# A transformer layer's MLP without GpSimd: the second matrix product taken one Strassen-Winograd product at a time over the whole contraction

## The chip, the cores and the metric

The kernel runs on one core of a Trainium2 chip. A core has a matrix engine (TensorE, PE in the rows), a vector engine (VectorE, DVE), a scalar engine (ScalarE, ACT), a general-purpose engine (GpSimd, POOL), a sync engine (SyncE, SP) that issues the DMAs here, an on-chip memory SBUF (128 partitions) and the accumulators PSUM (8 banks of 128 x 512 float32). Each engine works through its own instructions in order; engines wait for one another on semaphores. PEld in the rows is the matrix engine's weight load, which overlaps its matmuls. The metric is the device time of one execution in microseconds (us), the median of several runs.

## What is computed

One encoder layer on 1024 tokens of width 1024 in float32: neighbourhood attention, a layer norm, and then the part that the change touches:

```python
x   = layer_norm(DN_ALPHA * x + mix, ln1_g, ln1_b)
hid = square(relu(x @ w_ff1))                       # 1024 -> 4096
ple = sigmoid(x @ w_ple_gate) * (p @ w_ple_proj)
x   = layer_norm(DN_ALPHA * x + hid @ w_ff2 + ple, ln2_g, ln2_b)   # 4096 -> 1024
```

## The kernel before

Every float32 operand of a matmul is split in a high part (ScalarE copies it into the matmul's format) and a low part (VectorE subtracts: source minus high). Each product of two tiles is three matmuls (`PASSES`: high x high, high x low, low x high). So before every stretch of matmuls stand pairs "high on ScalarE, low on VectorE".

The function `mlp` has three stages, written out by hand for every engine, so each engine's order is that of the code.

The gate stage computes x @ w_ple_gate in 16 units (8 token tiles by 2 column halves) of 24 matmuls (`gate`, L2125). Per unit ScalarE takes the sigmoid (L1668) and VectorE does two operations (L1913, L1915). Beside it GpSimd forms the combinations of quarters of x that the next stage needs: `x_combinations`, 8 additions or subtractions of 128x512 for each of 4 chunks, 32 in all (L1548, L1558). Each result is split, low part on VectorE at L1881 (`x_low`). After unit 6, VectorE also makes the low parts of the second half of the gate weights (`low`, L1864, 128x1024 each), for which unit 8 waits.

The first product, x @ w_ff1, uses a Strassen-Winograd scheme: 7 products of quarter blocks instead of 8. It goes in 16 units; a unit has 7 products of 12 matmuls (L2165), in the order `UNIT_STEPS` = (1, 4, 5, 6, 2, 7, 3), where product 4 is that of the unit before. VectorE reads products out of PSUM and adds (`plus`, L1930), forms sums of the squared hidden blocks (`hidden_sum`, L1935), and makes the low parts of the next unit's weights (`w1_low`, L1887). GpSimd forms four 128x512 sums of weight blocks per unit (`sums_1_3`, `sums_2_4`, L1584 and L1548). Product 7 of a unit starts only after VectorE has read product 6 out of the same bank. The hidden blocks and their combinations go to DRAM (`S.hid`).

The second product, hid @ w_ff2, is again the 7-product scheme. The contraction of 4096 is cut in 4 "cubes" of 1024. Before, the order is cube by cube: step n is product `PRODUCTS[n % 7]` = (1, 2, 5, 3, 6, 7, 4) of cube n // 7, 28 steps of 4 token tiles (t) of 12 matmuls (L2203). Each step loads 1 MB of hidden blocks (`load_hidden`), splits one 128x2048 weight block (`w2_high` L1706, `w2_low` L1894) and four 128x512 hidden tiles (`hid_high` L1721, `hid_low` L1899). After every one of the 112 (step, tile) pairs VectorE adds the bank into y or `shared_sum` in SBUF (`add_product`, L2011, 4 first ones are copies, L1998). Products marked `CONTINUES` accumulate on the bank of the product before them. The weights are loaded once, 4 blocks of 1 MB per cube, and GpSimd forms the four weight sums per cube, 128x2048 each (L1548). At the last cube it also adds `shared_sum` to three quarters of y (`merge`, L1614, 12 operations).

The layer norm of tiles 0 to 3 starts when step 25 is added. The last two steps, 26 and 27, are interleaved by tile (`STEP_ORDER`). Tiles 4 to 7 use `statistics`, `variance`, `scale`, `offset`, and at the end gain and shift: the gain on VectorE (`times_gain`) or GpSimd, the shift mostly on GpSimd (L1647). VectorE's order at the end (L2063 to L2111) has additions of the last two steps between norm operations. The output goes out in 8 DMAs of one tile (512 KB).

VectorE's main loop of the second product:

```python
for n in range(STEPS2 - 2):
    w2_low(n + 1)
    for t in range(PAIR_TILES):
        hid_low(n + 1, t)
        if n == STEPS2 - 3 and t == PAIR_TILES - 1:
            w2_low(n + 2)
        add_product(n, t)
```

So during step n of the matrix engine VectorE prepares step n + 1. The parts of step n + 1 go into the buffers of step n - 1, so ScalarE's high parts wait until the matmuls of step n - 1 have read them.

Of the kernel before, what the change touches and what calls it, by code (L numbers as in the profile page):

```python
# [1147 lines left out]
def load_gate(sp, S, w_gate, half, i):  # L1148
# [32 lines left out]
STEP_AT = {step: at for at, step in enumerate(STEP_ORDER)}  # L1181

A11, A12, A21, A22, HS1, HS2, HS3, HS4 = range(8)
STAGED = {1: A11, 2: A12, 5: HS1, 3: HS4, 6: HS2, 7: HS3, 4: A22}


def mlp(nc, S, w_ff1, w_ff2, ln_g, ln_b, w_gate, out):

    with ExitStack() as ctx:
# [3 lines left out]
        def sem(name):  # L1193
# [18 lines left out]
        shared_sum = at("shared_sum", [P, PAIR_TILES, HALF], S.act_at + 32 * KB)  # L1212
        gain = at("ln2_gain", [P, D], S.act_at + 48 * KB)
        shift = at("ln2_shift", [P, D], S.act_at + 52 * KB)
        squares = at("ln2_squares", [P, 2, D], free + 48 * KB)

        last_w2 = at("w_ff2_last", [P, 2, KH4, HALF], free + 104 * KB, F32R)
        last_hid = at("hidden_last", [P, 2, 2, KH4, P], S.act_at + 56 * KB, F32R)
        hid_in = [S.raw[:, 0:2, :].rearrange("p a (b n) -> p (a b) n", n=HALF),
                  at("hidden_in", [P, KH4, HALF], free + 16 * KB)[:, :, :]]  # L1220
        w2_in = [S.raw[:, 2:4, :].rearrange("p a (b n) -> p (a b) n", n=HALF),
                 at("w_ff2_in_1", [P, KH4, HALF], free + 24 * KB)[:, :, :],
                 at("w_ff2_in_2", [P, KH4, HALF], free + 48 * KB)[:, :, :],
                 at("w_ff2_in_3", [P, KH4, HALF], free + 56 * KB)[:, :, :],
                 at("w_ff2_in_4", [P, KH4, HALF], S.act_at + 40 * KB)[:, :, :]]
# [35 lines left out]
        b_in = [sem(f"w_ff2_in{i}") for i in range(5)]  # L1261
# [3 lines left out]
        t2_lo = sem("w_ff2_lo_done")  # L1265
        s2_hi = sem("hidden_hi_done")
# [14 lines left out]
        last_ready = sem("out_last_ready")  # L1281
# [5 lines left out]

        X_STEPS = {1: (0, 1), 2: (2, 3), 3: (4,), 4: (5, 6), 5: (7, 8), 6: (9,), 7: (10,), 8: (11, 12), 9: (13,), 10: (14, 15)}

        EARLY_STEPS = (11, 12)  # L1290
# [66 lines left out]
        def hid_part(part, n, t):  # L1357

            if n % 2 == 0:
                return columns(early_slot(part, t) if t < 2 else wb_slot(part, 2 + t))  # L1360
            if n == STEPS2 - 1:
                return last_hid[:, part, t % 2] if t < 2 else xc[2][:, part, :, P * t:P * (t + 1)]
            if t < 2:
                return columns(wb_slot(part, 6 + t))
            return xc[2][:, part, :, P * (t - 2):P * (t - 1)]

        def w2_part(part, n):

            if n == STEPS2 - 1:
                return last_w2[:, part, :, :]  # L1370
# [4 lines left out]
        def w2_roles(b):  # L1375

            role = {A11: 0, A21: 1, A12: 2, A22: 3, "sum": 4}
            for _ in range(b):
                role = {A11: role[A11], A21: role[A22], A12: role["sum"], "sum": role[A12], A22: role[A21]}
            return role  # L1380

        def w2_loads(slot, b):

            return sum(w2_roles(i)[q] == slot for i in range(b + 1) for q in (A11, A12, A21, A22))
# [9 lines left out]
        def done2(n, t):  # L1394

            return STEP_AT[n, t] + 1

        def bank2(n, t):

            b, i = divmod(n, len(PRODUCTS))  # L1400
            return S.ps[PAIR_TILES * ((3 * b + CHAIN[PRODUCTS[i]]) % 2) + t][:, :]
# [6 lines left out]
        LAST_CUBE = CUBES - 1  # L1408
        MERGE_ORDER = (A22, A12, A21)

        OUT_ORDER = (0, 1, 2, 3, 4, 5, 7, 6)
        DVE_GAINS = 4

# [823 lines left out]
```

## Time and profile before

| | before |
|---|---|
| median of 3 runs | 1352.24 us (1350.94 to 1352.26) |
| the profiled execution | 1351.9 us, its span 1350.1 us |
| mean granted clock of the matrix engine | 0.972 |
| busy: PE, PEld, DVE, ACT, POOL | 1260.3, 1044.9, 912.5, 576.8, 372.3 us |
| first matmul of the gate stage, of the second product | 602.84, 1010.06 us |
| data moved | 174.89 MB, mean 130 GB/s |

The span is that of the profiled execution, from its first to its last instruction; 1.8 us lie around it. All stages named above stand in the last 750 us of the span. A stall of the matrix engine is shown in square brackets in the timeline, with the instruction that ended it.

### The profile page before, as it was taken

What the parts mean: (1) busy time and instruction counts of PE and PEld (TensorE: products, weight loads), DVE (VectorE), ACT (ScalarE), POOL (GpSimd) and SP (SyncE); (2) the same over time, 40 slices, a digit from 0 to 9 for tenths busy, and PEclk for the clock granted to TensorE, in tenths of its full rate; (3) what the DMA queues carried; (4) which work ended last, traced back from release to release, by engine and by line L of the source; (5) the groups of instructions that cost most, each with busy time, mean ns of one, the idle gap of its engine ahead of it and who ended that gap; (6) DMA issues with size and microseconds to landing.
All of it is one profiled execution on the core that took longest, in us unless ns stands there. A gap on an engine that the chain in (4) does not pass through costs nothing. (4 is left out here: it accounts for less than half of the span.)

```text
span 1350.1 us, 18089 instructions
## 1 busy us (share of the span) xinstructions
PE 1260.3 (93%) x5840; PEld 1044.9 (77%) x5840; DVE 912.5 (68%) x1665; ACT 576.8 (43%) x1103; POOL 372.3 (28%) x206
## 2 busy tenths in 40 slices
PE   4999999999999879979899999999999999999992
PEld 3778878878888667868688888888877888888872
DVE  3157766767677646568746666566649788787977
ACT  3145546546555651122324444444443333333352
POOL 0202112112111212129423322233205030222825
PEclk9999999999999899989999999999999999999996
DMA  7313222232223475444354444444456734545114
GB/s 177 83 45 75 69 56 52 66 81 51 66 51 94 147 214 139 136 166 158 125 164 160 143 158 163 142 145 160 164 197 231 273 126 164 167 140 184 63 63 125
DMA packets 120653, 174.89 MB, mean 130 GB/s; under 512 B 10112, under 2 KB 62464, under 8 KB 120576
## 3 DMA queue, kind: packets, MB, share of 16 engines
q1 hardware_dynamic: 120576, 173.95, 41.2%
q8 instruction: 37, 0.61, 0.2%
q14 instruction: 40, 0.33, 0.1%
HBM read 115.20 MB, written 50.52 MB: 123 GB/s over the span
## 5 line engine op out<-in xcount | busy, mean ns | idle before, releaser
L736 PE MATMUL bank<-act_T_hi,w_qkv_hi 128*128 128x512 f32 x384 | 153.7, 400 | 5.6 <-DVEq L689 4.6
L736 PE MATMUL bank<-act_T_hi,w_qkv_lo 128*128 128x512 f32 x384 | 153.8, 401 | 0.0
L736 PE MATMUL bank<-act_T_lo,w_qkv_hi 128*128 128x512 f32 x384 | 153.5, 400 | 0.0
L541 ACT ACTIVATE probabilities<-negated_scores,negated_max 128x384 f32<-128x384 f32 (+1 forms) x128 | 75.5, 590 | 172.0 <-DVE negated_max L669 171.5
L455 POOL TENSOR_TENSOR w_qkv_lo<-weight_raw,w_qkv_hi 128x1024 fp32r<-128x1024 f32 x22 | 52.9, 2403 | 298.0 <-ACT w_qkv_hi L504 298.0
L2165 PE MATMUL bank<-x_combination,weight_parts 128*128 128x512 f32 x480 | 112.9, 390 | 0.0
L2165 PEld LDWEIGHTS bank<-x_combination,weight_parts 128*128 128x128 f32 x480 | 90.1, 188 | 19.0 <-DVE hidden_staging L1930 0.4
L2125 PE MATMUL bank<-weight_parts,act_T_hi 128*128 128x512 f32 x256 | 83.9, 407 | 8.8 <-DVE weight_parts L1864 5.1
L736 PEld LDWEIGHTS bank<-act_T_hi,w_qkv_hi 128*128 128x128 f32 x384 | 73.4, 191 | 18.5 <-DVE w_qkv_lo L227 4.8
L2203 PE MATMUL bank<-weight_parts,weight_parts_early 128*128 128x512 f32 x336 | 80.5, 396 | 3.4 <-DVE weight_parts_early L1899 2.7
L736 PEld LDWEIGHTS bank<-act_T_hi,w_qkv_lo 128*128 128x128 f32 x384 | 73.5, 191 | 13.1
L736 PEld LDWEIGHTS bank<-act_T_lo,w_qkv_hi 128*128 128x128 f32 x384 | 73.5, 191 | 12.8
L2011 DVE TENSOR_TENSOR y<-bank,y 128x512 f32<-128x512 f32 x96 | 65.6, 683 | 23.6 <-PE bank L2203 23.5
L2203 PE MATMUL bank<-weight_parts 128*128 128x512 f32 x336 | 78.7, 390 | 0.4 <-DVE weight_parts L1899 0.4
L676 DVE RECIPROCAL total_reciprocal<-exp_total 128x1 f32<-128x1 f32 x128 | 21.0, 164 | 85.9 <-ACT probabilities L541 85.5
L2203 PEld LDWEIGHTS bank<-weight_parts,weight_parts_early 128*128 128x128 f32 x336 | 64.0, 191 | 17.9 <-issue 4.5
L1548 POOL TENSOR_TENSOR w_ff_in<-w_ff_in,w_ff_in 128x2048 f32<-128x2048 f32 x12 | 58.8, 4900 | 57.5 <-DMA w_ff_in<-in_w_ff 31.2
L650 DVE TENSOR_TENSOR prob_T_lo<-bank,prob_T_hi 128x256 fp32r<-128x256 f32 (+2 forms) x160 | 68.5, 445 | 8.1 <-ACT prob_T_hi L532 6.8
L2203 PEld LDWEIGHTS bank<-weight_parts 128*128 128x128 f32 x336 | 63.0, 188 | 13.8 <-issue 0.8
L2203 PE MATMUL bank<-x_combination,weight_parts 128*128 128x512 f32 x312 | 72.8, 389 | 0.0
L2203 PE MATMUL bank<-x_combination,x_combination 128*128 128x512 f32 x312 | 72.8, 389 | 0.0
L1751 ACT ACTIVATE hidden_staging<-hidden_staging 128x512 f32<-128x512 f32 x48 | 30.3, 632 | 90.7 <-DVE hidden_staging L1930 90.7
(226 smaller groups left out, 3092.4 us busy)
## 6 DMA issues: line engine op xcount, KB each, us to landing
hidden_combinations<-hidden_staging SPq DMA_DIRECT2D x112, 256.0 KB, 2.0
weight_raw<-in_w_ff SPq DMA_DIRECT2D x20, 1024.0 KB, 5.6
weight_raw<-hidden_combinations SPq DMA_DIRECT2D x14, 1024.0 KB, 5.3
hidden_in<-hidden_combinations SPq DMA_DIRECT2D x14, 1024.0 KB, 5.3
weight_raw<-in_na_w_qkv SPq DMA_DIRECT2D x24, 512.0 KB, 4.4
w_ff_in<-in_w_ff SPq DMA_DIRECT2D x12, 1024.0 KB, 7.8
x_tokens<-in_x SPq DMA_DIRECT2D x8, 512.0 KB, 11.3
bias_in<-rpb_rows SPq DMA_DIRECT2D x256, 6.0 KB
```

The costliest lines, as they stand in the source:

```text
L455: nc.gpsimd.tensor_tensor(w[1][:, slot, :, :], S.raw[:, kind, :].rearrange("p (k n) -> p k n", k=KC), w[0][:, slot, :, :].bitcast(F32), AL ...
L541: nc.scalar.activation(prob[:, u % 4, 0:n], score[:, u % 2, 0:n], ACT.Exp, scale=-1.0, bias=nmax[:, u % 4:u % 4 + 1], accum_out=total[:, u ...
L650: last = nc.vector.tensor_tensor(pT_part(pT[1], g, first, count), tile_ps[u % 2][:, at * P:(at + count) * P].rearrange("p (b q) -> p b q", ...
L676: nc.vector.reciprocal(recip[:, u % 4:u % 4 + 1], total[:, u % 4:u % 4 + 1]).then_inc(recip_done, 1)
L736: mm = nc.tensor.matmul(proj_ps[gi % 2][:, :], w[wp][:, (par + kind) % 2, k, :], S.act[ap][:, k, t * HALF:(t + 1) * HALF], start=(i == 0), ...
L1548: nc.gpsimd.tensor_tensor(dst, a, b, ALU.subtract).then_inc(count, 1)
L1751: nc.scalar.activation(stage[:, q, :], stage[:, q, :], ACT.Relu).then_inc(relu_done, 1)
L2011: nc.vector.tensor_tensor(dst, bank2(n, t), dst, ALU.add).then_inc(added, 1)
L2125: mm = nc.tensor.matmul(S.ps[6 + u % 2][:, :], S.act[ap][:, k, t * P:(t + 1) * P], wb_slot(wp, k), start=(k == 0 and n == 0), stop=(k == K ...
L2165: mm = nc.tensor.matmul(bank, w1_part(wp, u, p)[:, k, :], x_part(ap, p, k), start=(k == 0 and n == 0 and p in (1, 5, 6)), stop=(k == KH4 - ...
L2203: mm = nc.tensor.matmul(bank2(n, t), hid_part(ap, n, t)[:, k, :], w2_part(wp, n)[:, k, :], start=(k == 0 and i == 0 and p not in CONTINUES ...
```

## The change

GpSimd has no work left in `mlp`. Its 32 combinations of x go to VectorE, in three groups per chunk after the two operations of a gate unit (`x_first`, `x_second`, `x_third`, with `x_low` between them); units 6, 7, 14 and 15 have none. The first two low parts of unit 0's weights move from gate units 11 and 12 to 14 and 15. The four weight sums of each of the 16 units of the first product go to VectorE: `sums_1_3(u + 2)` at the end of an iteration, `sum_2(u + 1)` ahead of the reading of product 5, `sum_4(u + 1)` ahead of that of product 7. For unit 0 they stand among the low parts between the gate stage and the first unit.

The second product's order is turned round: product by product, and within a product the 4 cubes one after the other, accumulated in PSUM. Step n is product `PRODUCTS[n // 4]`, cube n % 4. A bank is read once per product and tile: 20 additions for products 2, 5, 3, 6, 7; product 1 is copied to `shared_sum` by ScalarE (4 copies); product 4 is read in 4 additions at the end. The weight blocks are loaded again for each product that needs them: 36 loads of 1 MB instead of 16 (`B_LOADS`), through 4 buffers, issued 3 steps ahead. The 16 weight sums of 128x2048 and the 12 merges of 128x512 go to VectorE, behind the second hidden tile of steps 6 to 21 and behind steps 4, 5 and 12. The last product (steps 24 to 27) goes tile by tile: a step is one token tile over all 4 cubes, 48 matmuls, with all four weight parts held; its hidden tiles are loaded in pieces of 512 bytes. The norm of tiles 0 to 3 is laid into steps 21 to 26, that of tiles 4 to 6 into the steps behind theirs. Gain and shift of all tiles are on VectorE, and the last tile goes out in two halves. The number of matmuls stays.

```diff
-STEP_ORDER = tuple((n, t) for n in range(STEPS2 - 2) for t in range(PAIR_TILES)) + tuple(
-    (STEPS2 - 2 + i, t) for i, t in ((0, 0), (0, 1), (1, 0), (0, 2), (1, 1), (0, 3), (1, 2), (1, 3)))
+LAST_FROM = STEPS2 - CUBES
+B_BLOCKS = {1: (A11,), 2: (A21,), 5: (A12, A11), 3: (A22,), 6: (A22, A21), 7: (A22, A12), 4: ()}
+B_LOADS = [(n, q) for n in range(LAST_FROM) for q in B_BLOCKS[PRODUCTS[n // CUBES]]]
...
 # SyncE
+                if n + 3 < LAST_FROM:
+                    for q in B_BLOCKS[PRODUCTS[(n + 3) // CUBES]]:
+                        load_w2(n + 3, q)
...
 # VectorE, gate stage
-                for j in X_STEPS.get(u, ()):
-                    x_low(j)
+                if x_ends(u) is not None:
+                    x_low(4 * x_ends(u) + 3)
+                if x_stage(u):
+                    k, i = x_stage(u)
+                    if i == 0:
+                        x_first(k)
+                    elif i == 1:
+                        x_second(k)
+                    else:
+                        x_third(k)
...
+            sum_2(0)
+            w1_low(0, 2)
+            w1_low(0, 3)
+            sum_4(0)
+            w1_low(0, 4)
+            w1_low(0, 5)
...
 # VectorE, first product
                     w1_low(0, 6)
+                    sums_1_3(1)
...
                     ahead(u + 1, 1)
+                    if u < LAST_UNIT:
+                        sum_2(u + 1)
...
+                    if u < LAST_UNIT:
+                        sum_4(u + 1)
...
+                    if u + 2 < UNITS1:
+                        sums_1_3(u + 2)
...
 # VectorE, second product
+            for n in range(STEPS2):
+                if n + 1 < LAST_FROM:
+                    w2_low(n + 1)
...
+                reads = n % CUBES == CUBES - 1 and CUBES <= n < LAST_FROM
+                for t in range(PAIR_TILES):
+                    if n + 1 < STEPS2:
+                        hid_low(n + 1, t)
+                    if t == 1:
+                        if n in (6, 7, 8, 9):
+                            b_sum_5(n - 6)
...
+                        elif n in (18, 19, 20, 21):
+                            b_sum_7(n - 18)
+                        if n in (15, 16, 17, 18):
+                            b_sum_4(n - 15)
+                    if reads:
+                        add_product(n, t)
+                if n in (4, 5, 12):
+                    merge({4: A22, 5: A12, 12: A21}[n])
...
+                if n >= LAST_FROM:
+                    t = PAIR_TILES + n - LAST_FROM
+                    add_product(n, t - PAIR_TILES)
+                    statistics(t, 0)
+                    variance(t)
...
 # TensorE, last product
+            for t in range(PAIR_TILES):
+                n = LAST_FROM + t
+                free_bank(4, t)
+                for b in range(CUBES):
+                    pe.wait_ge(last_lo, LAST_PARTS.index(b) + 1)
+                    pe.wait_ge(s2_lo, prepared(n, b))
+                    product(bank2(4, t), n, b, lambda part: last_part(part, b), False, b == CUBES - 1, 4)
```

## Rows read from the trace of the kernel before

**Rows 1.** Waits of PE by releaser, 500 to 1350 us: total us, times, longest us
```profile
PE bank L2125 <- DVE weight_parts L1864: 5.1, 2, 4.6
PE bank L2125 <- DVE weight_parts L1869: 3.6, 1, 3.6
...
PE bank L2203 <- issue: 6.8, 2, 5.3
...
PE bank L2165 <- DVE hidden_staging L1930: 1.9, 1, 1.9
```

**Rows 2.** Busy by windows: us, PE, PEld, DVE, ACT, POOL (instructions), PEclk, DMA share, GB/s
```profile
850.00:900.00 50.00, 50.00 (x223) 41.41 (x221) 30.51 (x43) 24.09 (x45) 12.30 (x9) 1.00 0.47 158
...
1045.00:1056.00 11.00, 11.00 (x50) 9.09 (x50) 11.00 (x15) 4.00 (x5) 0.00 (x0) 1.00 0.90 303
```

**Rows 3.** Timeline of PE, gate stage: start, us, what [idle before <- releaser]
```profile
602.84 0.79 PE L2125 MATMUL bank<-weight_parts,act_T_hi 128*128 128x512 f32 x1 [3.61 <-DVE weight_parts L1869]
...
611.18 0.56 PE L2125 MATMUL bank<-weight_parts,act_T_lo 128*128 128x512 f32 x1
...
656.02 0.76 PE L2125 MATMUL bank<-weight_parts,act_T_hi 128*128 128x512 f32 x1 [4.57 <-DVE weight_parts L1864]
...
659.14 0.48 PE L2125 MATMUL bank<-weight_parts,act_T_lo 128*128 128x512 f32 x1
```

**Rows 4.** Timeline of DVE, gate stage and start of the first product
```profile
625.21 1.78 DVE L1913 TENSOR_TENSOR hidden_staging<-hidden_staging 128x512 f32<-128x512 f32 x1
...
653.59 5.62 DVE L1864 TENSOR_TENSOR weight_parts<-weight_raw,weight_parts 128x1024 fp32r<-128x1024 f32 x3
...
702.18 0.69 DVE L1913 TENSOR_TENSOR hidden_staging<-hidden_staging 128x512 f32<-128x512 f32 x1 [4.02 <-ACT hidden_staging L1668]
...
711.04 1.28 DVE L1930 TENSOR_TENSOR hidden_staging<-bank,first_product 128x512 f32<-128x512 f32 x2
```

**Rows 5.** Timeline, start of the second product, POOL and DVE
```profile
1017.20 4.60 POOL L1548 TENSOR_TENSOR w_ff_in<-w_ff_in,weight_raw 128x2048 f32<-128x2048 f32 x1 [37.52 <-DMA w_ff_in<-in_w_ff]
1017.53 4.83 DVE L1899 TENSOR_TENSOR weight_parts<-hidden_in,weight_parts 128x512 fp32r<-128x512 f32 x1
```

**Rows 6.** Timeline of PE, last unit of the first product and the second product
```profile
1000.17 0.84 PE L2165 MATMUL bank<-x_combination,act_T_hi 128*128 128x512 f32 x2 [1.87 <-DVE hidden_staging L1930]
...
1010.06 5.60 PE L2203 MATMUL bank<-weight_parts,weight_parts_early 128*128 128x512 f32 x24
1015.50 5.60 PE L2203 MATMUL bank<-weight_parts 128*128 128x512 f32 x24
...
1037.70 4.58 PE L2203 MATMUL bank<-weight_parts,weight_parts_early 128*128 128x512 f32 x12 [2.01 <-DVE weight_parts_early L1899]
...
1325.91 5.46 PE L2203 MATMUL bank<-w_ff_last,x_combination 128*128 128x512 f32 x12 [5.28 <-issue]
```

**Rows 7.** Timeline of DVE, a norm without POOL work, and the last instruction
```profile
595.26 1.28 DVE L880 SCALAR_TENSOR_TENSOR x_tile<-x_tile,ln_mean_var,ln_gain 128x1024 f32<-128x1024 f32 x1
...
596.65 1.41 DVE L887 SCALAR_TENSOR_TENSOR x_tile<-x_tile,ln_mean_var,ln_shift 128x512 f32<-128x512 f32 x2
...
1344.74 1.23 DVE L2111 TENSOR_TENSOR y<-y,ln_shift 128x1024 f32<-128x1024 f32 x1
```

**Rows 8.** Groups by line: count | busy us, mean ns of one | idle before
```profile
L2011 DVE TENSOR_TENSOR y<-bank,y 128x512 f32<-128x512 f32 x96 | 65.6, 683 | 23.6 <-PE bank L2203 23.5
...
L1894 DVE TENSOR_TENSOR weight_parts<-weight_raw,weight_parts 128x2048 fp32r<-128x2048 f32 x2 | 4.6, 2292 | 6.5 <-ACT weight_parts L1706 6.5
```

**Rows 9.** DMA issues: count, KB each, median us from issue to landing
```profile
hidden_combinations<-hidden_staging SPq DMA_DIRECT2D x112, 256.0 KB, 2.0
weight_raw<-in_w_ff SPq DMA_DIRECT2D x20, 1024.0 KB, 5.6
...
weight_raw<-in_na_w_qkv SPq DMA_DIRECT2D x24, 512.0 KB, 4.4
...
w_ff_in<-in_w_ff SPq DMA_DIRECT2D x12, 1024.0 KB, 7.8
```

More of the change, by code:

```diff
@@ L1260, in mlp @@
         a_in = [sem(f"hidden_in{i}") for i in range(2)]
-        b_in = [sem(f"w_ff2_in{i}") for i in range(5)]
+        b_in = [sem(f"w_ff2_in{i}") for i in range(len(b_raw))]
         y_in = {q: sem(f"y_in{q}") for q in (A11, A12, A21, A22)}
@@ L1373, in w2_part, with last_part, raw_of, loads_of @@
             return xc[0][:, part, :, :]
[L1375 to L1384, printed above, removed]
+        def last_part(part, b):
+            return w2_buffer(part, {0: 0, 3: 1}[b]) if b in (0, 3) else last_w2[b][:, part, :, :]
+        def raw_of(n, q):
+            return b_raw[B_LOADS.index((n, q)) % len(b_raw)]
+        def loads_of(n, q):
+            j = B_LOADS.index((n, q))
+            return b_in[j % len(b_raw)], 16 * (j // len(b_raw) + 1)
+        def summed(p, b):
+            return B_SUMS.index((p, b)) + 1
+        def w2_source(n):
+            p, b = PRODUCTS[n // CUBES], n % CUBES
+            if p in (5, 6):
+                return b_sum[:, b, :, :]
+            return raw_of(n, {1: A11, 2: A21, 3: A22, 7: A12}[p])
         def y_block(q, t):
@@ L1516, in _ @@
                     load_hidden(1)
-                    load_w2(0, A21)
+                    load_w2(1, A11)
                     load_hidden(2)
@@ new lines, in _, with x_stage, x_ends @@
+            for h in range(2):
+                sp.wait_ge(out_ready, GROUPS + h)
+                sp.dma_start(token_half(out, GROUPS - 1, h), y[:, GROUPS - 1, h * HALF:(h + 1) * HALF]).then_inc(out_stored, 16)
+            sp.wait_ge(out_stored, 16 * (GROUPS + 1))
+        def x_stage(u):
+            if u in (GROUPS - 2, GROUPS - 1) or u >= GATE_TILES - 2:
+                return None
+            return divmod(u if u < GROUPS else u - 2, 3)
+        def x_ends(u):
+            return {3: 0, 6: 1, 11: 2, 14: 3}.get(u)
@@ L2201, in _, with product @@
+            def product(bank, n, t, weights, start, stop, p):
                 for k in range(KH4):
                     for i, (wp, ap) in enumerate(PASSES):
-                        mm = nc.tensor.matmul(bank2(n, t), hid_part(ap, n, t)[:, k, :], w2_part(wp, n)[:, k, :],
-                                              start=(k == 0 and i == 0 and p not in CONTINUES),
-                                              stop=(k == KH4 - 1 and i == 2), skip_group_check=p in CONTINUES)
+                        mm = nc.tensor.matmul(bank, hid_part(ap, n, t)[:, k, :], weights(wp)[:, k, :],
+                                              start=(start and k == 0 and i == 0), stop=(stop and k == KH4 - 1 and i == 2),
+                                              skip_group_check=p in CONTINUES)
@@ L2206, in _ @@
                 mm.then_inc(full2, 1)
+            for n in range(LAST_FROM):
+                p, b = PRODUCTS[n // CUBES], n % CUBES
+                pe.wait_ge(t2_lo, n + 1)
+                for t in range(PAIR_TILES):
+                    if b == 0:
+                        free_bank(p, t)
+                    pe.wait_ge(s2_lo, prepared(n, t))
+                    product(bank2(p, t), n, t, lambda part: w2_buffer(part, n), b == 0 and p not in CONTINUES,
+                            b == CUBES - 1, p)
```

597 lines of the change are left out of this document (281 added, 316 removed).

## The prediction

> **What bounds the kernel now.** I read the matrix engine's waits first, since it is busy for 1260 of the 1350 us: its idle time can be had back and little else. In the MLP they name VectorE, or "issue", where nothing shows [rows 1]. Then the windows, stage by stage: in the steady part of the first product the engine never stops and has its full clock, 2.4 GHz; VectorE is busy 30.5 of 50 us [rows 2]. Then the timelines, for what a stall costs. At the gate weights' second half 4.57 us are lost, and the clock restarts at the lower level: 7 matmuls take the 3.12 us from 656.02 to 659.14, where at the later pace they take 1.6 [rows 3]. That pace is 5.44 us per 24, or 0.2267 each [rows 6].
>
> Why is VectorE late there? Beside a GpSimd operation its 128x512 operation lasts 1.78 us, with GpSimd idle 0.69 [rows 4]; a hidden tile's low part started beside a 4.60 us GpSimd sum lasts 4.83 [rows 5], longer than that sum's remaining 4.3. Back to back a free one costs 0.60 (1.28 for two) [rows 4]. An addition that reads a bank has mean 683 ns over all 96, so GpSimd never held it [rows 8].
>
> The Trainium skill (SBUF — State Buffer, "Who interferes with whom") says so too: VectorE and GpSimd share a port pair, held for a whole instruction; a VectorE operation with two SBUF inputs waits for it, one with a single SBUF input does not. A split of bandwidth instead would make the 0.69 us operation about 1.4 beside GpSimd, not 4.83, and the stalls of the second product would have no cause in GpSimd: some 5 us of my sum would go. The trace agrees with the lock.
>
> **Part by part**, against the profiled execution, 1351.9 us, 0.3 under the median.
>
> Gate stage, start. The first low part, for which the engine waits 3.61 us [rows 3], overlaps GpSimd; without that 0.5 us goes. From 602.84 to 611.18, 16 matmuls start in 8.34 us [rows 3]; at full pace 3.6, so 4.7 us are lost, with a second gap of 0.5 [rows 1]. After the later restart only 1.5 were lost. With the second gap gone I take the later figure: 0.5 + 4.7 - 1.5 = -3.7; bounds -1.0 (gaps alone) and -4.2.
>
> Gate unit 8. VectorE gets 32 combinations, 32 x 0.60 = 19 us, up to 5 operations in a unit: with its own two 3.0 to 4.5 us against 5.44 of matmuls. Units 6 and 7 have none. The three low parts that began at 653.59 and took 5.62 us [rows 4] then take some 3.6, and start once ScalarE has the high parts, before unit 8 needs them. Gone: 4.57 + 1.5, less 0.2 for the fourth, which is just in time: -5.9; bounds -3 and -6.1. If this cover fails the stall comes back.
>
> Unit 0 of the first product. Here the moved work is not covered. The gate stage's last matmul ends about 0.8 before 702.18, at 701.4. Product 7 needs the bank of product 6 read, and wants to start 10.9 us after that, at 712.3; before, the second reading ends at 712.32, just in time [rows 4]. Now 15 VectorE operations stand between the unit-15 pair and that point: 6 low parts of unit 0, 2 of unit 1, 5 sums, 2 readings, of which the last is the one awaited. 15 x 0.60 = 9, plus 1.5 to 2 for handovers to ScalarE, from 703.5 on: 714 to 714.5. So +2 of stall, and the lower clock behind it, +1.7 as after the 1.87 us gap (from 1000.17 on [rows 6], 12 matmuls took 4.45 us instead of 2.7): +3.7; bounds 0 and +5.
>
> Steady units. 16 VectorE operations per 19.04 us become 20: 12 us uncontended. Queued behind `sum_2` are the readings of products 5 and 6, for which the matrix engine waits. From the unit's start: product 4's bank is full at 5.4, reading, two hidden sums, a low part and `sum_2` end at 8.5, reading 5 by 9.2, two sums and a low part 11.0, reading 6 by 11.7, wanted at 13.6. 1.9 us spare: nothing. The stall in the last unit [rows 1, 6] is behind a 2.29 us weight split that waits for its load and stays: 0, bounds -1 and +2.
>
> Second product. 28 x 48 matmuls at 0.2267 are 304.7 us; from 1010.06 that ends at 1314.8, before it ended at 1331.4 [rows 6]. The 16.6 us between are stalls and lower clock. 4.9 are lost by the tile of 1037.70, beside GpSimd sums: due at 1034.5, it is 3.2 late and takes 4.58 instead of 2.9 [rows 6]. Of the other 11.7 some 10 are in the last two steps, where the norm stands between additions in VectorE's order: one gap is 5.28, and the 12 matmuls behind it take 5.46 [rows 6]. After: removed are 88 of the 112 additions or copies on VectorE, at 0.60 about 53 us; added 16 sums at 2.29 [rows 8] are 37, 12 merges 7, so VectorE has less work than before. Its fullest steps (14, 16 to 18) hold 2.3 + 2.4 + 4.6 us and begin 1.9 after the matrix step: 11.2 against 10.9; the third and fourth hidden tile they delay are wanted 5 us later. The four ScalarE copies sit in step 3, 4.4 us full. The last product wants VectorE back for step 25's hidden tiles at about 8.4 us of 10.9, for step 26's at 18.4 of 21.8. Price 0, gain -16.5; bounds -16.6 and -8.
>
> Loads. 20 MB more. Steps 8 to 11 and 16 to 23 take 3.15 MB each. At 0.90 share 303 GB/s flowed [rows 2], so full share gives 337: 9.3 us of 10.9. `load_w2` also puts a new wait in SyncE's queue (a buffer's last reader on VectorE); behind it stands the next hidden load, which waits for about the same moment. The shortest window, a sum's second block in step 18, is 6.4 us against landings of 5.6 to 7.8 [rows 9]: up to 1.4 late, VectorE's spare 3.5. The 512-byte pieces cost no more: 512 KB so cut lands in 4.4 us [rows 9], two such in under 10.9. Price 0.
>
> Tail. Before, 18.7 us from the last matmul's end to the span's end. After: addition 0.7, half statistics 0.7, variance 0.2, first operation 1.2, reciprocal 0.2, two halves 1.4 [rows 7], a start of 0.1: 4.5. Then the store: 4.1 from the last VectorE end (1345.97) to the end with 512 KB; a 256 KB store lands in 2.0 [rows 9], another just ahead. I take 3.3: 7.8, so -10.9; bounds -10.1 and -12.
>
> Sum: -3.7 - 5.9 + 3.7 + 0 - 16.5 - 10.9 = -33.3. 1351.9 - 33.3 = 1318.6; with the 0.3, 1319.
>
> **Rivals.** The loads bound steps 8 to 23. If 3.15 MB flow at 250 GB/s they take 12.6 us, 1.7 over, x 12 = 20, less some 6 from loading ahead: 1333. For it: 7.8 us landings where loads queue. Against: 303 GB/s at 0.90 share. 10 in 100.
>
> VectorE's order bounds the first product, the one that ends slower. Place: `sum_2` and the low part ahead of the reading of product 6. It decides once the reading comes 1.9 us later than reckoned, at 13.6; each further us is paid in 15 units. At 2.5 us beyond, and some lower clock after the gaps, that is 37 + 5 = 42: 1361. For it: the order is in line, and each sum waits on ScalarE. Against: 12 us of work in 19. 3 in 100. A mild form, 0.5 us per unit, gives 1327: 7 in 100.
>
> GpSimd's part is not what stalls the gate and second product: the order of waits stays, only the tail (-10.9) and the last steps (-10) gain: 1331. Against: [rows 4, 5]. 7 in 100. Unit 0 has no stall: 1315, 20 in 100, within the forecast.
>
> **Numbers.** Forecast, 1312 to 1326: 72 in 100. The rivals hold 27 (10, 3, 7, 7), a change that does nothing 1. The range takes the forecast with both its bounds on unit 0 and the tail, and the milder rivals: 1312 to 1333. Faster by over 0.2% (what a measurement can tell): 0.96; same 0.01; slower 0.03.
>
> **What would show it.** Right: no POOL instruction after 600 us; all VectorE low parts of 128x512 at 0.69; no PE gap at gate unit 8; a gap of about 2 us before unit 0's product 7; the second product in 305 us; 8 us behind the last matmul. Wrong: PE gaps ended by a DMA or by L1930 in unit after unit, or a DMA share of 1.0 over steps 16 to 23.

## The result, and the profile after

The changed kernel takes 1315.25 us (median of 4 runs, 1313.6 to 1317.6), the kernel before 1351.83 us beside it: a ratio of 0.9732, with a 95% interval of 0.9715 to 0.9748. The forecast was 1319.0. The profiled execution took 1315.8 us, its span is 1314.0 against 1350.1.

First the waits of the matrix engine, from 595 us to the end (columns as in [rows 1]):

```profile
PE bank L2232 <- DVE hidden_staging L1983: 3.4, 2, 2.0
PE bank L1104 <- DVE x_tile L887: 3.1, 1, 3.1
PE bank L2192 <- DVE weight_parts L1817: 3.1, 1, 3.1
```

The "issue" row is gone, and L2192 (the gate, once L2125) has one wait left, the first. The reading of the first product's banks now names two gaps where [rows 1] had one.

The timeline of the matrix engine, gate stage and first product:

```profile
600.83 0.80 PE L2192 MATMUL bank<-weight_parts,act_T_hi 128*128 128x512 f32 x1 [3.07 <-DVE weight_parts L1817]
...
606.54 0.42 PE L2192 MATMUL bank<-weight_parts,act_T_lo 128*128 128x512 f32 x1
...
703.43 3.02 PE L2232 MATMUL bank<-x_combination,weight_parts 128*128 128x512 f32 x12 [1.37 <-DVE hidden_staging L1983]
...
991.34 0.73 PE L2232 MATMUL bank<-x_combination,act_T_hi 128*128 128x512 f32 x2 [2.01 <-DVE hidden_staging L1983]
```

Between the first of these rows and the third no gap is listed: the stall of 4.57 us of [rows 3] has gone. The second shows where the pace at the gate's start becomes full.

The end of the kernel, from the last matmuls on:

```profile
1303.19 2.88 PE L2264 MATMUL bank<-x_combination,hidden_parts_odd 128*128 128x512 f32 x12
1306.11 0.69 DVE L2065 TENSOR_TENSOR y<-bank,y 128x512 f32<-128x512 f32 x1 [4.70 <-PE bank L2264]
...
1309.28 1.41 DVE L2177 SCALAR_TENSOR_TENSOR y<-y,ln_mean_var,ln_shift 128x512 f32<-128x512 f32 x2
```

The groups by line that answer to [rows 4, 5, 8] (1040 to 1270 us), the operations that GpSimd held before among them:

```profile
L1850 DVE TENSOR_TENSOR weight_parts<-hidden_in,weight_parts 128x512 fp32r<-128x512 f32 x22 | 14.2, 685 | 0.0
L2065 DVE TENSOR_TENSOR y<-bank,y 128x512 f32<-128x512 f32 x20 | 13.8, 688 | 5.3 <-PE bank L2264 5.3
L1854 DVE TENSOR_TENSOR w_ff_sums<-w_ff_in,w_ff_sums 128x2048 f32<-128x2048 f32 x6 | 13.6, 2286 | 0.0
```

The hidden tile's low part, 4.83 us in [rows 5], now has a mean of 0.685. The addition that reads a bank did not change (0.683 to 0.688).

To say where the 36.1 us of span went, I cut both traces at the same marks and compare each stretch with its matmuls at full pace (0.2267 us each, [rows 6]):

| stretch | before | after | difference | reckoned |
|---|---|---|---|---|
| up to the last transposes before the MLP (597.46, 595.98) | | | -1.5 | 0 |
| first wait of the gate | 3.61 | 3.07 | -0.5 | -0.5 |
| gate stage, first matmul to first product (384 matmuls, 87.05 at full pace) | 98.5 | 89.9 | -8.7 | -9.1 |
| first product (304.7 at full pace) | 308.7 | 310.6 | +1.9 | +3.7 |
| second product (304.7 at full pace) | 321.3 | 304.8 | -16.5 | -16.5 |
| last matmul to the end | 18.7 | 7.9 | -10.8 | -10.9 |

The first line isn't the change's: in the kernels of this study, whose code is the same up to there, these transposes start anywhere between 595.13 and 598.50.

### The profile page after: what moved, and what is told of

It reads as the page before. It is cut to its first block and busy times, and to the rows that moved or that the text cites. A ratio compares the mean times of both kernels' runs of the same rounds, so it can differ in the third digit from the quotient of the medians.

```text
span 1314.0 us, 17894 instructions
## 1 busy us (share of the span) xinstructions
PE 1247.0 (95%) x5840; PEld 1037.6 (79%) x5840; DVE 857.7 (65%) x1711; ACT 579.2 (44%) x1107; POOL 107.2 (8%) x73
## 5 line engine op out<-in xcount | busy, mean ns | idle before, releaser
L2232 PEld LDWEIGHTS bank<-x_combination,weight_parts 128*128 128x128 f32 x480 | 90.0, 188 | 20.4 <-DVE hidden_staging L1983 1.8
L2192 PE MATMUL bank<-weight_parts,act_T_hi 128*128 128x512 f32 x256 | 81.1, 398 | 3.1 <-DVE weight_parts L1817 3.1
L2264 PE MATMUL bank<-weight_parts,weight_parts_early 128*128 128x512 f32 x312 | 73.0, 389 | 0.0
L2264 PE MATMUL bank<-weight_parts 128*128 128x512 f32 x312 | 73.0, 389 | 0.0
L2264 PE MATMUL bank<-x_combination,hidden_parts_odd 128*128 128x512 f32 x312 | 73.0, 389 | 0.0
L2264 PEld LDWEIGHTS bank<-x_combination,hidden_parts_odd 128*128 128x128 f32 x312 | 58.6, 188 | 12.1
L2264 PEld LDWEIGHTS bank<-weight_parts 128*128 128x128 f32 x312 | 58.6, 188 | 12.1
L2264 PEld LDWEIGHTS bank<-x_combination,weight_parts 128*128 128x128 f32 x312 | 58.6, 188 | 12.2
L2264 PEld LDWEIGHTS bank<-weight_parts,weight_parts_early 128*128 128x128 f32 x312 | 58.6, 188 | 12.2
## 6 DMA issues: line engine op xcount, KB each, us to landing
x_tokens<-in_x SPq DMA_DIRECT2D x8, 512.0 KB, 11.5
```

What stands on the lines that cost most here:

```text
L2192: mm = nc.tensor.matmul(S.ps[6 + u % 2][:, :], S.act[ap][:, k, t * P:(t + 1) * P], wb_slot(wp, k), start=(k == 0 and n == 0), stop=(k == K ...
L2232: mm = nc.tensor.matmul(bank, w1_part(wp, u, p)[:, k, :], x_part(ap, p, k), start=(k == 0 and n == 0 and p in (1, 5, 6)), stop=(k == KH4 - ...
L2264: mm = nc.tensor.matmul(bank, hid_part(ap, n, t)[:, k, :], weights(wp)[:, k, :], start=(start and k == 0 and i == 0), stop=(stop and k == ...
```

## Experiments

Each kernel is the kernel before or the changed one with one thing altered. Times are medians, 3 rounds; the kernel before, beside them, took 1350.7 in the first four and 1352.2 us in all others.

**1. The engine alone, in the second product.** The kernel before, with GpSimd's 16 sums and 12 merges of the second product given to VectorE; its step order and its 112 readings stay.

```diff
-            for b in range(CUBES):        # GpSimd: sums; then the 12 merges
...
                 for t in range(PAIR_TILES):
                     hid_low(n + 1, t)
+                    if t == 1 and n % 7 < 4:
+                        second_sum(n // 7, (5, 7, 6, 4)[n % 7])
...
                     add_product(n, t)
+                if n in (21, 22, 24):
+                    merge(MERGE_ORDER[(21, 22, 24).index(n)])
```

> The kernel before with one thing changed: the 16 weight sums of the second product and the 12 merges are on VectorE instead of GpSimd. Its order of cubes, its 112 readings, the gate stage, the first product, the last product and the norm stay as before, with GpSimd where it was. Port theory (what held VectorE was GpSimd's work beside it): the stall by the tile of 1037.70 goes, and the small ones later; the second product is 4 to 7 us shorter, the time 1345 to 1348. Rival (what matters is that 88 readings are gone): VectorE now holds 24 copies or additions a cube round and the sums as well, 2.3 + 2.4 + 4.6 + 2.4 = 11.7 us in steps of 10.9, so the second product is no shorter or some us longer, the time 1351 to 1358.

Measured 1344.3 us, ratio 0.9953 (0.9938 to 0.9968): 6.5 us less, within the 4 to 7 of the port theory. The matrix engine's timeline:

```profile
1025.72 5.60 PE L2208 MATMUL bank<-x_combination,x_combination 128*128 128x512 f32 x24
1031.16 5.60 PE L2208 MATMUL bank<-weight_parts,weight_parts_early 128*128 128x512 f32 x24
1036.60 5.60 PE L2208 MATMUL bank<-weight_parts 128*128 128x512 f32 x24
...
1299.44 3.00 PE L2208 MATMUL bank<-w_ff_last,hidden_last 128*128 128x512 f32 x12 [1.56 <-issue]
...
1318.91 5.46 PE L2208 MATMUL bank<-w_ff_last,x_combination 128*128 128x512 f32 x12 [5.32 <-issue]
```

The three gaps at the 1037.70 tile of [rows 6] are gone, though VectorE has more to do and the readings are all there. The two gaps in the last steps stand as before. The second product is 315.0 us (1009.40 to 1324.37), so 6.3 of the 16.5 us come from GpSimd's sums and merges, and 10.2 from the rest of the change. The trace says where these stand (columns as in [rows 2]):

```profile
1009.40:1292.20 282.80, 282.80 (x1249) 234.27 (x1248) 232.98 (x267) 109.13 (x137) 0.00 (x0) 1.00 0.49 171
```

Steps 0 to 25 take 282.9 us, from 1009.40 to 1292.28, which is 1248 matmuls at full pace: nothing is lost in them, cube by cube and with every step's readings. All of the 10.2 us are in the last two steps. So in the steps before them, once GpSimd's work there is gone, the turned order and the fewer readings bring the matrix engine nothing; what the rest of the change brings is in the last two, where the norm stood between the additions. The fourth experiment shows that the last product needn't go tile by tile for it either. Whether the fewer readings, the place of the norms or GpSimd's gains and shifts, which this kernel keeps (14.3 us of its work lie between 1292.3 and 1324.3), account for the 10.2 was not taken apart.

**2. The second half of the change alone.** Gate stage and first product as before, with GpSimd's combinations and sums (its code for them taken over word for word); all behind them as changed.

```diff
+        @block.gpsimd                           # combinations of x, sums of w_ff_in
...
+                for j in X_STEPS.get(u, ()):    # VectorE, gate stage
+                    x_low(j)
...
-                    sums_1_3(1)                 # VectorE, first product
...
-                        sum_2(u + 1)
...
-                        sum_4(u + 1)
...
-                        sums_1_3(u + 2)
```

> The changed kernel with the gate stage and the first product as before: GpSimd makes the 32 combinations of x and the sums of w_ff_in. The second product, the norm and the tail are as changed. By the sum of the prediction with the measured tail, second product and tail are worth 16.5 + 10.8 = 27.3 us: 1324.5. So gate stage and first product together should be worth 9 us on this chip (1324.5 against about 1315.3); had the second half of the change done more through some later effect of the first half, this kernel would stand nearer to 1330.

Measured 1323.9 us, ratio 0.9801 (0.9785 to 0.9818). Its second product is 304.8 us and its tail 7.9, as in the changed kernel, and the old waits of the gate are back:

```profile
PE bank L2230 <- DVE weight_parts L1872: 5.0, 2, 4.5
PE bank L2230 <- DVE weight_parts L1877: 3.7, 1, 3.7
...
PE bank L2270 <- DVE hidden_staging L2028: 1.9, 1, 1.9
```

So the parts of the change add up: 8.6 us for gate stage and first product by the medians, 7.5 by the spans, against 9 expected.

**3. Why are there two gaps left in the first product?** The order of VectorE altered where it stands ahead of the awaited reading (ScalarE's in the last unit too).

```diff
                 if u == 0:
                     w1_low(0, 6)
-                    sums_1_3(1)
-                if mine:
+                if mine and 0 < u < LAST_UNIT:
                     ahead(u + 1, 0)
...
                     plus(stage[:, A21, :], bank_b(u), first_product[:, u % 2, :], evacuated)
+                    if u == 0:
+                        sums_1_3(1)
+                        ahead(1, 0)
+                        ahead(1, 1)
+                        sum_2(1)
+                    if u == LAST_UNIT:
+                        ahead(u + 1, 0)
```

> The changed kernel with VectorE's order altered in two places: in unit 0 of the first product the sums of unit 1 and its first low parts come behind the reading of product 6 instead of ahead of it, and in the last unit the split of the second product's first weight comes behind that reading on ScalarE and VectorE alike. Theory (both gaps are readings queued behind other work on VectorE): the 1.37 us gap of unit 0 and the 2.01 us gap of the last unit with the lower clock behind it (1.7) go: 1.4 + 3.7 = 5 us less, 1310. Rival (the banks are waited for because ScalarE's half of the work, or the matrix engine itself, is late): the gaps stay or move by a product, 1315; and the weight split, now later, could stall the first tile of the second product by up to 3 us, 1318.

Measured 1309.96 us, ratio 0.9698 (0.9677 to 0.9720). Both gaps are gone, the weight split causes none:

```profile
PE bank L1119 <- DVE w_o_lo L1061: 4.9, 1, 4.9
PE bank L1104 <- DVE x_tile L887: 3.1, 1, 3.1
PE bank L2201 <- DVE weight_parts L1819: 3.1, 1, 3.1
```

From the gate's first matmul to the second product's first it takes 393.5 us (601.71 to 995.23), the changed kernel 400.4. Of the 6.9 us between them the two gaps and the clock behind the second are 5.1, what product 7 of unit 0 loses beyond its listed gap 0.5 (below), and the remaining 1.3 is again the clock, at the gate's start (below too), which this edit doesn't touch. This version is the fastest of all here, though its interval just touches the changed kernel's.

**4. Tile by tile, or step by step.** The changed kernel, its last product in the usual order, its norms behind the last step.

```diff
-            for n in range(LAST_FROM):          # TensorE
+            for n in range(STEPS2):
...
-            for t in range(PAIR_TILES):
-                n = LAST_FROM + t
-                free_bank(4, t)
-                for b in range(CUBES):
-                    ...
...
+            for t in range(PAIR_TILES, GROUPS): # VectorE
+                add_product(STEPS2 - 1, t - PAIR_TILES)
+                statistics(t, 0)
+                variance(t)
+                if t - 1 >= PAIR_TILES:
+                    scale(t - 1)
+                    offset(t - 1)
+                    gain_and_shift(t - 1)
```

> The changed kernel with the last product step by step, as the other products: each of its four cubes goes over all four tiles, each tile's bank is read once after the last cube, and its weights go through the usual buffers. No GpSimd, same numbers of matmuls and readings otherwise. Theory (going tile by tile lets three of the four tiles' additions, statistics and norms run beside matmuls): four banks become full within the last 10.9 us instead of one in 10.9, so three more additions, statistics and norms (some 3.4 us of VectorE a tile) press behind the end: the tail is 14 to 15 us instead of 7.9, time about 1322. Rival (the readings once per product did it all): tail within 1 us of 7.9, time 1315 to 1316.

Measured 1325.4 us, ratio 0.9800 (0.9777 to 0.9822): 10.1 us more than the changed kernel, where 6 to 7 were expected. VectorE at the end:

```profile
1303.36 0.69 DVE L2052 TENSOR_TENSOR y<-bank,y 128x512 f32<-128x512 f32 x1 [1.06 <-PE bank L2239]
...
1308.97 0.69 DVE L2052 TENSOR_TENSOR y<-bank,y 128x512 f32<-128x512 f32 x1
...
1314.56 0.68 DVE L2052 TENSOR_TENSOR y<-bank,y 128x512 f32<-128x512 f32 x1
...
1321.62 1.42 DVE L2152 SCALAR_TENSOR_TENSOR y<-y,ln_mean_var,ln_shift 128x512 f32<-128x512 f32 x2
```

Its second product takes 304.8 us as well (1003.97 to 1308.76), so nearly all of the difference is behind the last matmul. The additions follow one another at 5.6 us, not at the 3.4 that I had counted, since each tile's gain and shift (two of 1.23 us) and a wait for ScalarE stand between them; the tail is 17.6 us against 7.9. So the tail's gain rests on the order of the last product, given this order of the norms. How much a better order of these norms would have given back was not tried.

**5. Is it the lock, or the chain of waits?** The changed kernel, with work on GpSimd that nobody waits for, in steps 4 to 22: two subtractions of an unused area from itself a step, and then two memsets in their place.

```diff
+        @block.gpsimd
+        def _(pool):
+            area = first_product[:, :, :]
+            for n in range(4, 23):
+                pool.wait_ge(t2_lo, n + 1)
+                for i in range(2):
+                    pool.wait_ge(xc_raw, 8 * CUBES + 2 * (n - 4) + i)
+                    nc.gpsimd.tensor_tensor(area, area, area, ALU.subtract).then_inc(xc_raw, 1)
```

> The changed kernel with work on GpSimd that nobody waits for: from step 4 to step 22 of the second product two subtractions 128x1024 a step of an SBUF area, unused by then, from itself (the result is not used). Port theory: each takes 2.4 to 3 us and in that time no VectorE operation with two SBUF inputs runs, so such VectorE operations last up to 3 us instead of 0.69 and in the fullest steps (9.3 us of VectorE in 10.9) 5 to 6 us of lock are over by some 4 us: stalls return in the second product, 15 to 50 us slower. Rival (GpSimd's work was a link in the chain of waits, not a hindrance): nothing, within 1 us of 1315.

> The same with memsets of the area, 128x1024, in place of the subtractions: GpSimd is as present in the program and waits and signals the same, but reads nothing. If it is reading two inputs from SBUF that shuts VectorE out, the time stays at 1315 and VectorE's 128x512 operations stay at 0.69 us; if any GpSimd access to SBUF does it, they grow and the time too, by the share of time that the memsets take.

Measured 1320.2 us (ratio 0.9778, 0.9754 to 0.9801) with the subtractions, 1315.0 (0.9726, 0.9710 to 0.9743) with the memsets. Groups by line with the subtractions, 1040 to 1270 us (the POOL row from 1000):

```profile
L1577 POOL TENSOR_TENSOR first_product<-first_product 128x1024 f32<-128x1024 f32 x38 | 85.5, 2249 | 587.6 <-DVE weight_parts L1849 523.8 <-DVE x_combination L1849 62.3
...
L1859 DVE TENSOR_TENSOR weight_parts<-hidden_in,weight_parts 128x512 fp32r<-128x512 f32 x20 | 28.1, 1447 | 0.0
...
L2074 DVE TENSOR_TENSOR y<-bank,y 128x512 f32<-128x512 f32 x20 | 13.6, 680 | 0.2 <-PE bank L2273 0.2
```

and with the memsets:

```profile
L1577 POOL MEMSET first_product<- 128x1024 f32 x38 | 36.3, 956 | 624.7 <-DVE weight_parts L1849 542.9 <-DVE x_combination L1849 80.7
...
L1859 DVE TENSOR_TENSOR weight_parts<-hidden_in,weight_parts 128x512 fp32r<-128x512 f32 x20 | 12.9, 685 | 0.0
```

The low part's mean doubles beside subtractions and stays beside memsets; the addition from a bank stays in both. No dependency ties these operations together, so a chain of waits is out. A doubled mean alone could still be a split of bandwidth, in which no operation of 0.69 us would last beyond 1.4. Single ones do:

```profile
1124.21 4.57 POOL L1577 TENSOR_TENSOR first_product<-first_product 128x1024 f32<-128x1024 f32 x2 [4.41 <-DVE weight_parts L1849]
...
1125.25 1.78 DVE L1859 TENSOR_TENSOR weight_parts_early<-weight_raw,weight_parts_early 128x512 fp32r<-128x512 f32 x1
1126.96 0.68 DVE L2074 TENSOR_TENSOR y<-bank,y 128x512 f32<-128x512 f32 x1
1127.56 1.78 DVE L1859 TENSOR_TENSOR weight_parts<-weight_raw,weight_parts 128x512 fp32r<-128x512 f32 x1
```

Each of the two low parts ends about half a us after the subtraction beside which it began (at 1126.5 and 1128.8), and the addition between them takes 0.68 while the second subtraction runs. That is the lock.

The price is another matter: 4.9 us, and I had expected 15 to 50. The lock was a little shorter than reckoned (two of 2.25 us a step, not of 2.4 to 3), but the main error is in what comes of it. Four short gaps of the matrix engine do, 4.5 us together, the first at 1190.85 in step 17. As I read it, VectorE may fall some us behind before the matrix engine stands still, and the lighter steps let it catch up.

The Trainium skill (SBUF — State Buffer, "Who interferes with whom") names VectorE operations with two SBUF inputs as those that wait, and only for a GpSimd instruction that reads SBUF. The runs agree: 1447 ns in the mean with two inputs, 680 with one from a bank, and 685 with two beside memsets.

**6. How near are the loads to a bound?** First, copies of 1 MB from device memory to device memory beside the loads of 12 heavy steps, one or two a step.

```diff
+                if n in (5, 6, 7, 8) or 13 <= n <= 20:
+                    for i in range(2):          # or 1
+                        ...
+                        sp.dma_start(scratch[j], src).then_inc(out_stored, 16)
```

> The changed kernel with one further copy of 1 MB (from w_ff2 in device memory to an unused place in device memory) in each of 12 steps of the second product, queued on SyncE ahead of the step's own loads, at the steps whose loads are heaviest (3.15 MB becomes 4.2 MB). Nothing waits for the copies but the end of the program. Theory (the loads have about a tenth to spare): at 344 GB/s, seen in the fullest stretch after, 4.2 MB take 12.2 us of 10.9, 1.3 over, 12 times, less about 8 from loading ahead: 5 to 12 us slower, 1320 to 1327. Rival (the loads are far from a bound, as the 391 GB/s seen in a stretch without stores allows: 10.7 us): within 2 us of 1315.

> The same with two further copies of 1 MB in each of the 12 steps: 5.25 MB a step. Theory: 15.3 us at 344 GB/s, 4.4 over, 12 times, less 8: about 45 us slower, 1360. At 391 GB/s it would be 13.4, 2.5 over, 12 times, less 8: 22 us slower, 1337. Rival (loads do not bound even then, since buffers are refilled two to three steps ahead): 1315 to 1320. With the run of one copy this gives the price of a further MB once the queues are full, about 2.7 to 3.1 us.

Measured 1371.4 us (ratio 1.0162, 1.0133 to 1.0190) and 1497.2 (1.1068, 1.1045 to 1.1091). The first MB of each step cost (1371.4 - 1315.25) / 12 = 4.7 us, the second (1497.2 - 1371.4) / 12 = 10.5, over three times what 1 MB takes at the 344 GB/s below. The loads' own landings show the queue behind such a copy (with one a step, 1040 to 1280 us):

```profile
w_ff_in<-in_w_ff SPq DMA_DIRECT2D x22, 1024.0 KB, 13.7
```

against 7.7 without it. That is a price of copies within device memory, and says nothing of the spare of the loads. I had chosen the wrong transfer, so the question was put again with further loads into an unused SBUF area, 1 MB and 1.5 MB in each of 9 steps:

```diff
+                if n in (5, 6, 7, 8) or 13 <= n <= 17:
...
+                    src = bass.AP(w_ff2.tensor, w_ff2.offset, [[D, P], [UNIT * D, KH4], [1, HALF]])
...
+                    sp.dma_start(extra[:, :, :], src).then_inc(out_stored, 16)
+                    src = bass.AP(w_ff2.tensor, w_ff2.offset, [[D, P], [UNIT * D, 2], [1, HALF]])
+                    sp.dma_start(first_product[:, :, :], src).then_inc(out_stored, 16)
```

> The copies from device memory to device memory cost some 10.5 us of time for each MB (1497.2 - 1371.4 over 12 copies), three times what a load of the kernel takes of the queue, so they did not measure the loads' spare. Here the changed kernel gets one further load of 1 MB from w_ff2 into an unused SBUF area, of the kernel's own form, in each of 9 steps of the second product (3.15 MB becomes 4.2 MB); nothing else reads it. Theory (full share is 344 GB/s): 12.2 us of 10.9, 1.3 over, 9 times in two stretches, less up to 8 of loading ahead: 2 to 10 us slower, 1317 to 1325. Rival (391 GB/s, as in one stretch): 10.7 of 10.9, within 1 us of 1315. If loads were already at their bound (the prediction's rival of 250 GB/s), 4.2 us for each of the 9: 1340 and more.

> The same with 1.5 MB more in each of the 9 steps (a second load of 512 KB into another unused area): 4.7 MB a step. At 344 GB/s 13.7 us of 10.9, 2.8 over, 9 times, less 8: 17 us slower, 1332. At 391 GB/s 12.1, 1.2 over, 9 times, less 8: 1316 to 1322. At 250 GB/s: 1350 and more.

Measured 1316.1 us (0.9731, 0.9714 to 0.9747) and 1316.9 (0.9730, 0.9709 to 0.9752): neither is told from the changed kernel. The windows with 1.5 MB more (columns as in [rows 2]):

```profile
1066.00:1077.00 11.00, 11.00 (x50) 9.12 (x49) 7.24 (x8) 4.00 (x5) 0.00 (x0) 1.00 1.05 387
1077.00:1088.00 11.00, 11.00 (x50) 9.11 (x49) 7.02 (x7) 4.00 (x5) 0.00 (x0) 1.00 1.05 387
1088.00:1099.00 11.00, 11.00 (x50) 9.11 (x49) 9.51 (x11) 4.00 (x5) 0.00 (x0) 1.00 1.05 387
```

and two of the fullest of the changed kernel:

```profile
1208.00:1219.00 11.00, 11.00 (x50) 9.13 (x49) 9.06 (x10) 4.00 (x5) 0.00 (x0) 1.00 0.95 331
1219.00:1230.00 11.00, 11.00 (x51) 9.09 (x50) 9.68 (x8) 5.86 (x7) 0.00 (x0) 1.00 0.96 344
```

The queue carries 387 GB/s, not the 337 that I had scaled from [rows 2], and the matrix engine is busy 11.00 of 11.00 us all the same. The rival of a bound at 250 GB/s falls. And a DMA share of 1.0, which I had named as a sign of being wrong, is none by itself: in these windows, steps 5 to 8, it is 1.05, and the matrix engine doesn't wait.

**7. VectorE's spare in the steady units.** Five further operations in each of units 1 to 14, ahead of the reading of product 6.

```diff
                         ahead(u + 1, 2)
+                        for i in range(5):
+                            dve.wait_ge(xc_raw, 8 * CUBES + 5 * (u - 1) + i)
+                            nc.vector.tensor_scalar(S.ps[7][:, :], S.ps[6][:, :], 1.0, None, ALU.mult).then_inc(xc_raw, 1)
                     dve.wait_ge(full[6], u + 1)
```

> The changed kernel with five further VectorE operations of 128x512 (a copy from one unused PSUM bank to another, scaled by 1; the result is not used) in each of units 1 to 14 of the first product, ahead of the reading of product 6. Theory (that reading is the tightest point, 1.4 us ahead of need in the trace after, 1.9 by the prediction): five take 3.0 to 3.5 us, so a gap of 1.6 to 2.1 us ahead of product 7 in each of 14 units, 22 to 29 us; if the lower clock follows each gap, as after the 1.87 us one before, 1.7 more each, to 53 in all: 1337 to 1368. Rival (ScalarE's handovers or another reading set the pace, and VectorE has 7 us idle in a unit of 19): the five operations fall into idle time, 1315 to 1320.

Measured 1356.8 us, ratio 1.0036 (1.0023 to 1.0049): 41.6 us more than the changed kernel. The waits:

```profile
PE bank L2235 <- DVE hidden_staging L1983: 30.7, 16, 2.0
```

Less the gaps of unit 0 and of the last unit (1.38 and 1.55 here), 27.8 us stand in 14 units, 1.98 each. Five back to back take 3.54 us (744.25 to 747.79), so the spare was about 1.5, as the trace after shows: its reading of product 6 ends at 873.48 and product 7 starts at 874.92. VectorE is idle several us in each of these units, and that helps nothing: the place in its order decides. More is lost than the gaps: by the profiles the first product takes 353.5 us instead of 310.6. Three units one after another:

```profile
748.52 4.61 PE L2235 MATMUL bank<-x_combination,weight_parts 128*128 128x512 f32 x12 [1.98 <-DVE hidden_staging L1983]
...
771.44 0.74 PE L2235 MATMUL bank<-x_combination,act_T_hi 128*128 128x512 f32 x2 [1.98 <-DVE hidden_staging L1983]
772.02 0.40 PE L2235 MATMUL bank<-x_combination,act_T_lo 128*128 128x512 f32 x1
...
792.80 4.61 PE L2235 MATMUL bank<-x_combination,weight_parts 128*128 128x512 f32 x12 [1.98 <-DVE hidden_staging L1983]
```

and the granted clock behind the first two gaps (columns as in [rows 2]):

```profile
750.50:752.50 2.00, 2.00 (x6) 1.57 (x5) 0.00 (x0) 0.00 (x0) 0.00 (x0) 0.50 0.00 0
...
773.40:776.00 2.60, 2.60 (x13) 2.14 (x12) 0.69 (x1) 0.74 (x2) 0.00 (x0) 1.00 0.00 0
```

Twelve matmuls take 4.61 us in the first and the third, where the full pace gives 3.02 with the gap before it (row of 703.43 above); in the second two take 0.74 and the third follows at the full distance. From gap to gap it is 21.3 us or 22.9, and the longer ones stand behind the gaps of units 1, 2, 4, 6 and so on to 14: eight times 1.6 us, 13 for the clock. The 14 gaps with what goes at each restart are 2.3 each (21.3 against 19.04), 32. Taken off are some 2 us, since the last unit's gap is shorter than in the changed kernel and no lower clock follows it.

## Why the prediction was right, step by step

**Gate, start: mis-sized.** The overlap with GpSimd went as reckoned (3.61 to 3.07), the second gap too. But I took 1.5 us of lower clock behind the restart and 2.8 were lost: the granted clock is 0.50 of full up to 606.5, and the pace is full from 606.54 on, 13 matmuls later. The same gap of 3.07 us in the reordered kernel is followed by a full pace from about 604.75, 1.5 us lost. So the term was not wrong in kind; it needed both ends as its range, and the bounds that I gave (-1.0 to -4.2) held them. Measured: -0.5 for the wait and -1.9 for the rest, the second gap and the clock together; -2.4 against -3.7.

**Gate unit 8: right.** No gap, and nothing of the 0.2 kept back for the fourth part. Above full pace, 384 matmuls lose 11.5 us before and 2.8 after. Before, 5.1 of them are gaps and 4.1 the clock at the start, so about 2.2 lay behind the gap of unit 8 and not 1.5: -6.8 where -5.9 was reckoned. The two errors of the gate stage nearly cancel.

**Unit 0 of the first product: the stall right, the clock not.** The gap is where it was said to be, ahead of product 7, and ends with the second reading:

```profile
692.85 0.69 DVE L1835 TENSOR_TENSOR weight_parts_early<-weight_sum,weight_parts_early 128x512 fp32r<-128x512 f32 x1
...
695.02 0.69 DVE L1835 TENSOR_TENSOR weight_parts<-weight_sum,weight_parts 128x512 fp32r<-128x512 f32 x1 [0.76 <-ACT weight_parts L1620]
...
702.09 1.28 DVE L1983 TENSOR_TENSOR hidden_staging<-bank,first_product 128x512 f32<-128x512 f32 x2
```

The fifteen operations take 10.5 us, from 692.85 to 703.37 (reckoned 10.5 to 11), and begin 2.2 behind the first product's first matmul, at 690.68 (reckoned 2.1). Product 7, due at 690.68 + 10.88 = 701.56, starts at 703.43: 1.9 us late, reckoned 2. The row lists 1.37 of it as one gap; some 0.3 are in two pauses ahead of it that are too short to be listed, and the rest is that a matmul's end is shown later than the next one's start. But no lower clock followed: the 12 matmuls behind the gap take 3.02 us, and the granted clock there is 1.00. Reckoned +3.7, measured +1.9. The clock term had been carried over from another gap as if it always came; the seventh experiment shows that it comes or doesn't.

**Steady units: right.** No gap in units 1 to 14; the spare was 1.44 us, reckoned 1.9. The rival that ends slower is real in its mechanism, and the seventh experiment is that rival made true: 3.5 us of VectorE work in that place, and the kernel is slower than before (1356.8). It was not met by 1.4 us a unit.

**Last unit: as said.** The gap stays, 2.01 against 1.87, and the third experiment shows that it needn't: the weight split stood ahead of the readings, not behind a load that the matrix engine needs at that time.

**Second product: right to the tenth.** The first experiment shares its 16.5 us out: 6.3 for GpSimd's sums and merges, 10.2 for the norms, the readings and GpSimd's part in the norms together; I had said 4.9 by the tile of 1037.70 and some 10 in the last two steps. The fullest steps of VectorE, 9.3 us of work by the sum, show as 9.1 to 9.7 busy in windows of 11, and no gap comes of them. What I had not seen is that fewer readings are no condition for this in steps 0 to 25: the first experiment loses nothing there with all of them.

**Loads: right, with the wrong margin.** Reckoned at 9.3 of 10.9 us; half as much again cost nothing that can be measured. The full-share figure taken from one window with 0.90 share was 13% low.

**Tail: right.** 4.5 us of work was reckoned ahead of the stores and 3.3 for them: the last operation ends at 1310.69, 4.6 behind the last matmul's end at 1306.07, and the span ends 3.3 later.

The sum was -33.3 and the spans differ by 36.1. Of the 2.8 us between them 1.8 are unit 0's clock term, 1.5 lie ahead of the MLP where nothing was changed, and the gate stage and the tail give back 0.5. The medians stand 3.7 apart (1319.0, 1315.25); the other 0.9 is how the profiled executions stand to their medians.

One agreement is luck. The rival "unit 0 has no stall" named 1315, the very time that was measured, and it was wrong: the stall of 1.9 us is there. The time came to 1315 mostly because the clock behind it stayed up and 1.5 us were gained ahead of the MLP, where nothing was changed.

## What to carry to other kernels

An engine that runs in order is judged at the places where another waits for it, by what stands ahead of that point, and not by its busy share; that is how both gaps of the first product were found and taken away for 5 us. A two-input GpSimd operation on SBUF can hold up VectorE's two-input ones for its whole length (a memset doesn't; no other kind of GpSimd operation was run), so sums are cheaper on VectorE itself, as long as its order has room at the awaited points. In a norm at the end, the last product should finish tile by tile: 7.9 us stand behind the last matmul instead of 17.6. And a change of several parts should be tried part by part: of the second product's two gains, the one in steps 0 to 25 needs only the sums moved off GpSimd, not the new order.

## What the hardware showed that was not expected

The clock behind a gap is no fixed price. In the seventh experiment gaps of the same length, at the same place in every unit, are followed by the lower level (1.2 GHz, a granted clock of 0.50) in eight units of fourteen, from unit 2 on in every second one. After 1.37 us in unit 0 there was none, nor after gaps of 1.55 and 1.74 in the last unit (in the seventh experiment and in the run with 1 MB more); after 1.87 and 2.01 there was. After 3.07 it lasted 3.0 us in one kernel and 5.7 in another, with the same matmuls before it.

A copy of 1 MB within device memory on the loads' queue cost 4.7 us a piece with one in each of 12 steps, and a second one 10.5 more; a further load of 1 MB into SBUF in each of 9 steps cost nothing that can be measured.

A GpSimd memset of 128x1024 takes 0.96 us and leaves VectorE's operations as they are; a subtraction of that size takes 2.25 and stretches those of 0.69 to as much as 1.45 us in the mean of a group, and single ones to 2.38 (the one from 1104.53 on).
